# Conditioned hybrid layer: the first norm's row weighing, tile turns and column sums put in another order

## The reference

```
cond = silu(c)                                   # one vector of 1024
mod  = cond @ ada_w + ada_b                      # 6*1024 columns
sh1, sc1, g1, sh2, sc2, g2 = split(mod, 6)
hn   = rmsnorm(x, norm1_g) * (1 + sc1) + sh1     # x is (2048, 1024)
u    = hn @ w_in                                 # gate branch and x branch
x_br = causal_dwconv(x_br, conv_w, conv_b)       # 4 taps along the tokens
r, i = sigmoid(xb @ wa + ba), sigmoid(xb @ wx + bx)   # 8 blocks of 128 channels
h_t  = a_t * h_(t-1) + sqrt(1 - a_t^2) * i * xb  # a = exp(-8 r softplus(-lambda))
```

## Time and profile before

| | us |
|---|---|
| median of 3 runs | 1262.37 |
| the three runs | 1267.21, 1262.37, 1259.74 |
| the profiled execution, its own time | 1262.1 |
| its span in the trace | 1260.4 |

### The profile page before, as it was taken

The page is one execution under the profiler, slowest core; times in us unless marked ns, Lnnn a source line. Parts: engine busy times, 40 slices in busy tenths (PEclk is TensorE's granted clock), DMA queues, the critical chain, the costliest instruction groups (busy, mean ns, idle before and its releaser), DMA issues. The chain is left out here.

```text
span 1260.4 us, 18928 instructions
## 1 busy us (share of the span) xinstructions
PE 1093.1 (87%) x4857; PEld 850.4 (67%) x4858; DVE 768.6 (61%) x1198; ACT 650.0 (52%) x900; POOL 611.9 (49%) x665
## 2 busy tenths in 40 slices
PE   2797999999999997379999992599799999999991
PEld 2686788888888885368888871476466666766660
DVE  3477866667657664536677778356456655656541
ACT  3988766776677666322222212255556655555541
POOL 0061726637447340022567767146555655666553
PEclk9788999999999999689999995699999999999996
DMA  9550334433343312661445627857687887776751
GB/s 362 194 193 29 107 102 135 154 117 121 118 156 118 117 51 83 220 231 69 152 179 189 234 118 267 271 191 252 222 297 245 288 299 245 261 250 231 246 168 51
DMA packets 130871, 231.00 MB, mean 183 GB/s; under 512 B 24104, under 2 KB 91776, under 8 KB 129296
## 3 DMA queue, kind: packets, MB, share of 16 engines
q1 hardware_dynamic: 88976, 118.15, 28.2%
q0 software_dynamic: 23632, 62.49, 13.5%
q10 hardware_dynamic: 18224, 49.90, 11.6%
HBM read 175.87 MB, written 91.31 MB: 212 GB/s over the span
## 5 line engine op out<-in xcount | busy, mean ns | idle before, releaser
L1687 PE MATMUL po<-w_dn,e_ah 128*128 (+1 forms) x312 | 147.1, 616 | 16.9 <-issue 8.9
L1666 PE MATMUL pl<-w_hi,e_xh 128*128 (+1 forms) x312 | 140.9, 452 | 11.8 <-DVE e_xl L1577 6.3
L1210 PE MATMUL po<-wo_hi,b_yh 128*128 128x512 f32 x256 | 105.0, 410 | 28.0 <-DVE wo_lo L1024 28.0
L1668 PE MATMUL pl<-w_hi,e_xl 128*128 (+1 forms) x312 | 124.7, 400 | 0.0
L1667 PE MATMUL pl<-w_lo,e_xh 128*128 (+1 forms) x312 | 124.0, 397 | 0.0
L558 DVE SCALAR_TENSOR_TENSOR XB<-xu,v_cols,XB 128x512 f32<-128x512 f32 x96 | 90.1, 939 | 43.2 <-ACT XB L336 39.5
L1687 PEld LDWEIGHTS po<-w_dn,e_ah 128*128 128x128 f32 x312 | 57.9, 195 | 80.0 <-issue 80.0
L1377 POOL TENSOR_TENSOR e_ob<-e_obs,e_fg 128x1024 f32<-128x1024 f32 x38 | 91.1, 2397 | 32.2 <-ACT e_obs L1495 32.2
L674 PE MATMUL pg<-hT_hi,wg_hi 128*128 128x512 f32 x256 | 103.1, 403 | 0.0
L1211 PE MATMUL po<-wo_lo,b_yh 128*128 128x512 f32 x256 | 101.6, 397 | 0.0
L1212 PE MATMUL po<-wo_hi,b_yl 128*128 128x512 f32 x256 | 101.6, 397 | 0.0
(11 more groups left out here) (287 smaller groups left out, 2637.4 us busy)
## 6 DMA issues: line engine op xcount, KB each, us to landing
e_xg<-hn_slots ACTq DMA_DIRECT2D x40, 512.0 KB, 5.4
e_xa<-x_slots ACTq DMA_DIRECT2D x38, 512.0 KB, 3.8
stg<-in_ada_w_dram POOLq DMA_DIRECT2D x32, 512.0 KB, 4.2
w_raw<-in_moe_w_down_dram SPq DMA_DIRECT2D x16, 1024.0 KB, 7.3
w_raw<-in_moe_w_gate_dram SPq DMA_DIRECT2D x32, 384.0 KB, 4.3
w_raw<-in_moe_w_up_dram SPq DMA_DIRECT2D x32, 384.0 KB, 5.7
n_ada<-in_ada_w_dram ACTq DMA_DIRECT2D x4, 2048.0 KB, 18.4
hn_slots<-in_x_dram SPq DMA_DIRECT2D x16, 512.0 KB, 5.4
```

Of the source, the lines that this page charges most:

```text
L1210: nc.tensor.matmul(po[u][:, hcols], yh[u][:, tok], wo_hi[:, k, hcols], start=(k == 0), stop=False)
L1666: nc.tensor.matmul(gu[:], xh[:, tok], hi, start=(k == 0), stop=False)
L1668: last = nc.tensor.matmul(gu[:], xl[:, tok], hi, start=False, stop=(k == KD - 1))
L1687: last = nc.tensor.matmul(dst, ah[:, k * P:(k + 1) * P], rows, start=(k == 0), stop=(k == KF - 1))
```

## The change

Nothing is computed otherwise; calls change places in four of the engines' lists, and one overlay moves.

- DVE: the eight `weigh` are spread less: 1 to 7 stand among the diagonals 0 to 4 and are all done before diagonal 5; before, 5 to 7 stood among the diagonals 5 to 9. The diagonals 14 and 15 go into the first pass of the channel loop.
- PE: the column sums stand behind turn 4 (before: turn 9). Turns 5 to 7 follow, then the first projection; 8 and 9 behind it, 10 and 11 behind the second, 12 to 15 behind the first gate projection.
- ACT: `squares` and `evacuate` take the places that this asks for; group 0 is finished after `squares(8)` (before: `squares(13)`), the squares 13 to 15 and evacuations 10 to 15 lie in the first pass, groups 2 and 3 both at its end.
- There are four diagonals in a ring instead of two, over `macc` instead of `XBh`. So POOL, whose sums write `macc`, waits for turn 15 before its first one. It did not wait for turns before.

```diff
-        vrow, diag = over("v_rows", [VROWS * KD, P], "mtmp"), over("n_diag", [P, 2, P], "XBh")
+        vrow, diag = over("v_rows", [VROWS * KD, P], "mtmp"), over("n_diag", [P, NDIAG, P], "macc")
...
             def diagonal(it):
...
-                if it >= 2:
-                    dve.wait_ge(turned, it - 1)
+                if it >= NDIAG:
+                    dve.wait_ge(turned, it - NDIAG + 1)
...
@@ ACT @@
+            squares(7)
+            squares(8)
             finish_group(0)
-            for it in range(14, NT):
-                evacuate(it - 4)
+            for it in range(5, 8):
+                evacuate(it)
+            for it in range(9, 12):
                 squares(it)
             finish_group(1)
-            evacuate(12)
-            evacuate(13)
+            act.wait_ge(s_b, 1)
+            nc.scalar.activation(sp_t[:, 3], sp_t[:, 2], ACT.Ln).then_inc(s_a, 1)
...
+            evacuate(8)
+            evacuate(9)
+            squares(12)
...
                     if begins and h == 0:
-                        evacuate(14)
-                        evacuate(15)
+                        squares(13)
+                        evacuate(10)
+                        evacuate(11)
+                        squares(14)
...
-                        finish_group(2)
+                        squares(15)
+                        for it in range(12, NT):
+                            evacuate(it)
...
                     if begins and h == 0:
+                        finish_group(2)
                         finish_group(3)
@@ POOL @@
             load(0, 0)
             load(0, 1)
+            pool.wait_ge(turned, NT)
@@ PE @@
-            for it in range(10):
+            for it in range(5):
                 turn(it)
             pe.wait_ge(acc_step, KD)
...
-            turn(10)
-            turn(11)
+            for it in range(5, 8):
+                turn(it)
...
-                            turn(12 + 2 * n)
-                            turn(13 + 2 * n)
+                            turn(8 + 2 * n)
+                            turn(9 + 2 * n)
...
                         project("g", pg[n], (h * NH + n) * NB).then_inc(g_mm, 1)
+                        if h == 0 and n == 0 and not at_least(j, 1):
+                            for it in range(12, NT):
+                                turn(it)
                         gates(h, n)
```

More of the change, by code:

```diff
@@ L94, in norm_and_lru @@
         macc = sb("macc", [P, NB])
+        XT = ("A", "T", "M", "GE", "TI")
+        XR, NDIAG = len(XT), 4
         acc = over("n_acc", [P, 2 * D], "stg")
-        vrow, diag = over("v_rows", [VROWS * KD, P], "mtmp"), over("n_diag", [P, 2, P], "XBh")
-        XT = ("A", "T", "M", "GE", "TI")
+        vrow, diag = over("v_rows", [VROWS * KD, P], "mtmp"), over("n_diag", [P, NDIAG, P], "macc")
         xt = [over("n_x_" + n, [P, D], n) for n in XT]
@@ L262, in _ @@
                 squares(it)
-            for it in range(4, 14):
-                evacuate(it - 4)
[L265 to L281, removed]
+            evacuate(0)
+            squares(4)
+            evacuate(1)
+            convert("x", 0)
+            evacuate(2)
+            squares(5)
+            evacuate(3)
+            convert("g", 0)
+            act.wait_ge(gw_in, 32)
+            nc.scalar.activation(gwh[:], gw[:], ACT.Copy).then_inc(gw_hi_done, 1)
+            squares(6)
+            act.wait_ge(vec_ready, 1)
+            nc.scalar.activation(sp_t[:, 0], lam, ACT.Abs).then_inc(s_a, 1)
+            act.wait_ge(s_a, 1)
+            nc.scalar.activation(sp_t[:, 1], sp_t[:, 0], ACT.Exp, scale=-1.0).then_inc(s_a, 1)
+            evacuate(4)
+            squares(7)
+            squares(8)
             finish_group(0)
-            for it in range(14, NT):
-                evacuate(it - 4)
+            for it in range(5, 8):
+                evacuate(it)
+            for it in range(9, 12):
                 squares(it)
             finish_group(1)
-            evacuate(12)
-            evacuate(13)
+            act.wait_ge(s_b, 1)
+            nc.scalar.activation(sp_t[:, 3], sp_t[:, 2], ACT.Ln).then_inc(s_a, 1)
+            act.wait_ge(cond_ready, 1)
+            nc.scalar.activation(xu[:, 0, 0:CONV - 1], zero[:], ACT.Copy).then_inc(halo_ready, 1)
+            evacuate(8)
+            evacuate(9)
+            squares(12)
             def gates_out(c, n, j):
@@ L463, in _ @@
             nc.vector.tensor_copy(vec[:].rearrange("p r k -> p (r k)"), pg[0][:, 0:VROWS * KD]).then_inc(vec_ready, 1)
+            weigh(1)
             diagonal(0)
-            weigh(1)
+            weigh(2)
             diagonal(1)
-            weigh(2)
+            weigh(3)
             diagonal(2)
+            weigh(4)
+            weigh(5)
             diagonal(3)
-            weigh(3)
             diagonal(4)
+            weigh(6)
+            weigh(7)
             low_weights("x", 0)
-            weigh(4)
             diagonal(5)
+            low_weights("g", 0)
+            low_gates(0)
             diagonal(6)
+            columns()
+            diagonal(7)
+            finish_group(0)
+            for it in range(8, 12):
+                diagonal(it)
             dve.wait_ge(s_a, 2)
             nc.vector.tensor_scalar(sp_t[:, 2], sp_t[:, 1], 1.0, None, ALU.add).then_inc(s_b, 1)
[L478 to L489, removed]
+            finish_group(1)
             diagonal(12)
             diagonal(13)
-            finish_group(1)
-            diagonal(14)
-            diagonal(15)
             dve.wait_ge(s_b, 1)
@@ L584, in body @@
                     low_xb(c, 0)
+                    if begins and h == 0:
+                        diagonal(14)
                     if before:
@@ L588, in body @@
                     if begins and h == 0:
-                        finish_group(2)
+                        diagonal(15)
                     if h == 1 and not last:
@@ L652, in turn @@
                 for k in range(KD):
-                    last = nc.tensor.matmul(pt[it % 2][:, k * P:(k + 1) * P], xt[it % XR][:, k * P:(k + 1) * P], diag[:, it % 2],
+                    last = nc.tensor.matmul(pt[it % 2][:, k * P:(k + 1) * P], xt[it % XR][:, k * P:(k + 1) * P], diag[:, it % NDIAG],
                                             start=True, stop=True)
```

3 lines of the change are left out of this document (1 added, 2 removed).

## The result

| | before | after |
|---|---|---|
| median of 13 runs each, same chip, us | 1259.74 | 1265.49 |
| lowest to highest | 1252.02 to 1267.21 | 1260.35 to 1272.26 |
| the profiled execution, its own time | 1262.1 | 1272.26 |
| its span | 1260.4 | 1270.5 |

The ratio after to before is 1.0055, 95% interval 1.0031 to 1.0079: the kernel became slower, by 6.9 us (3.9 to 10.0); the two medians lie 5.75 us apart. I had predicted 1261.2 us and no measurable difference. The time of 1265.49 us lies inside the range that I gave (1255.5 to 1268), but the kernel moved where I had said that it would not: the interval excludes 1, and the loss stands at about the 0.5% that I had called too little to measure. The chance that I gave to slower was 0.08.

What follows compares the result with a forecast made beforehand. ACT was taken to bound the head's end: groups 2 and 3 end at 118.0 instead of 119.05, plus 24.6 us gives 142.6 for the second pass; 1262.1 less 1.0 is 1261.1, forecast 1261.2 us, range 1255.5 to 1268.

Steps and rivals of the forecast that it cites:

- What bounds the kernel: PE sets the pace from the second pass on; ACT bounds the head's end, with 24.6 us from 119.05 to 143.6.
- Start of group 0: ACT begins group 0 at 48.2 instead of 66.93, 18.7 us earlier.
- First projection: PE's first projection, behind turn 7 at 3.7 us, starts at 60.1, 13.2 us earlier than 73.30.
- First gates: PE's first gates start at 97.4 as turns 14 and 15 hang on evacuation 12; 1.5 of 13.2 us are left.
- Groups 2 and 3: ACT's groups run from 101.9 to 118.0, with POOL beside DVE, against 119.05 before: 1.0 us earlier.
- the taps at 1.7 times: Bound: DVE slowed beside POOL by the taps' ratio in groups 2 and 3; ACT ends near 124.2, kernel 1267.3 us.
- The tail: From ACT's end of group 3 to the second pass, 24.6 us as before, giving 142.6 instead of 143.6.
- POOL's sums: POOL's first pass ends at 121 to 125, hidden if before 129.1, some 4 us of cover.
- rival 2: POOL is late for `mod_sum`, ending at 136.6; second pass 7.5 us later, kernel 1269.6 us; chance 0.06.
- Rivals 1 and 3: 1: early projection's 13.2 us stay, 1249 us, chance 0.11. 3: sums stay put as condition rows come late, 1266, chance 0.05.
- The rule of the Trainium skill: GpSimd contends with VectorE instructions of two SBUF inputs or two-port mode; taken alone, it gives ACT's end at 119.3.
- The clock: PE's idle gaps before turns 7 and 14 bring the lower clock; full clock there wins 1.8 us each, 1257.5 us.

Runs made afterwards that it cites:

- e2: After, with the four diagonals over `TR` instead of `macc` and POOL's sums begun early, without a wait for turns; ratio to before 1.0012.
- e3: After, with the diagonals over `TR` and POOL's sums waiting for group 1's low parts instead of turn 15; ratio to before 1.0027.
- e4: Before, with one line added: POOL waits for turn 15 before its first sum; ratio to before 0.9979.
- e7: After, with evacuations 5, 12, 13, squares 15 and diagonals 14, 15 moved earlier, diagonals over `TR`, POOL's sums early without the wait; ratio to before 0.9961.
- e8: The closed-up order of turns with diagonals over `TR`, but POOL's sums wait for turn 15 as in after; ratio to before 1.0004.
- e10: The closed-up order of turns with diagonals over `TR`, POOL's sums waiting for group 0's low parts; ratio to before 0.9975.
- e5: After, with the diagonals over `TR` instead of `macc` but POOL still waiting for turn 15; ratio to before 1.0065.
- e1: After, with POOL's first pass cut to 8 of 512 columns behind its first step; only the head is read, ratio to before 1.0091.
- e6: After, with the additions of POOL's first pass cut to 8 columns, scalings at full width; only the head is read, not timed.
- e9: After, with POOL's first-pass scalings behind the first cut to 8 columns, additions at full width; only the head is read, not timed.

## Why the prediction was wrong, step by step

- *What bounds the kernel*: right. PE is busy for all of 150 to 200 us in after too, so what the head loses is kept. The head's 4.8 us (at the second pass's first gates) stand beside 6.9 (3.9 to 10.0) in the ratio. For e2 it is 0.3 beside 1.5, for e3 1.9 beside 3.4, for e4 0.3 beside -2.6, for e7 -6.75 beside -4.9, for e8 0.5 beside 0.5, for e10 -4.4 beside -3.1, each within the ratio's interval. e5's 3.6 beside 8.2 (5.2 to 11.2) is outside, which stays open. The two profiled executions differ by 10.1 us; the 5.3 beyond the head come after 165 us. From the second pass's first gates to the end before needs 1100.4 us and after 1105.7, but e5, which is as slow as after, 1096.0, and e4, in before's order, 1106.3: that looks like scatter from one execution to the next.
- *Start of group 0*: predicted 48.2, measured 48.23.
- *First projection*: predicted 60.1, measured 59.77, with turn 7 at 3.75 us (taken: 3.7).
- *First gates*: predicted 97.4, measured 95.97. Most of the 1.4 us comes from the twelve small decay operations, priced at 3.45 us by a row of before with POOL at work beside them; in after, with POOL idle, they take 1.71 (82.14 to 83.85). That turn 14 hangs on evacuation 12 fits the trace: its row names DVE's reciprocal, but that is tile 15's, diagonal 14 had been done since 87.96, and ACT's evacuations 12 and 13 ran from 89.62. In e7, with evacuation 12 further ahead, turn 14 follows turn 13 without idle and the first gates are at 91.15.
- *Groups 2 and 3*: this is the step that failed, in one term. Their place was right (predicted 101.9 for the start, measured 100.65), the gap before the second gates went as said. But the price of POOL beside DVE was taken as a factor 1.19, less half for slack, which put 1.5 us on the 116.5 worked out for ACT alone. The factor is 1.88 for the subtractions and 1.97 for the scalings; the slack that DVE has without the sums, 1.4 us in e1, is used up (no gap from 101.63 to 115.3). The sums cost 6.5 us, from 116.06 in e1 to 122.57, where 118.0 had been predicted. e1's 116.06 beside the 116.5 says that the rest of the working was sound.
- *Why I took 1.19*: the 821 ns are the mean of a window that has one whole addition of POOL in it (82.45). DVE's timeline of before over that window had the price, had I looked at single rows: beside the addition two subtractions take 2.38 us, in front of it two take 1.33.

```profile
80.55 1.33 DVE L451 TENSOR_TENSOR hT_lo<-n_zT,hT_hi 128x512 fp32r<-128x512 f32 x2 [1.73 <-ACT hT_hi L257]
...
82.57 2.38 DVE L451 TENSOR_TENSOR hT_lo<-n_zT,hT_hi 128x512 fp32r<-128x512 f32 x2
```

The row nearer in kind was in my bounds: the taps at 1.7 times, which gave 124.2 and 1267.3. The window of those taps in before has POOL busy for 3.56 of 3.90 us:

```profile
93.20:97.10 3.90, 3.90 (x18) 3.19 (x17) 3.83 (x4) 0.55 (x1) 3.56 (x4) 1.00 0.40 134
```

Three operations beside a POOL in full work are closer to the new stage than eight subtractions beside a POOL that waits for a DMA. I took the value near the milder row because it was the same line of the code, where it should have been the one with the same neighbour.
- *The tail*: a second, smaller term that was off. I kept 24.6 us from the tanh to the end of the fourth gates, that is 23.1 to their start. Measured 24.4, 1.3 us more. All kernels in the new order have 24.2 to 24.5 there, wherever their first sums lie (e1: 24.26), and the two in the old order, before and e4, 23.1 and 23.0. POOL's second pass also begins sooner behind the tanh, 4.1 us in after (126.71) and 8.8 in before (127.87), and DVE's taps and scan are longer beside it; that this is the cause no run shows. With the 4.6 us at the tanh it makes the 5.9 by which the second pass missed its predicted start (142.6, measured 148.5). DVE's timeline of after, then of before:

```profile
131.00 3.83 DVE L564 SCALAR_TENSOR_TENSOR XB<-xu,v_cols,XB 128x512 f32<-128x512 f32 x3 [2.54 <-ACT XB L341]
...
136.91 3.38 DVE L553 TENSOR_TENSOR_SCAN M<-A,T 128x1024 f32<-128x1024 f32 x1
```

```profile
127.50 2.96 DVE L558 SCALAR_TENSOR_TENSOR XB<-xu,v_cols,XB 128x512 f32<-128x512 f32 x3 [2.59 <-ACT XB L336]
...
133.22 2.28 DVE L547 TENSOR_TENSOR_SCAN M<-A,T 128x1024 f32<-128x1024 f32 x1
```

- *POOL's sums and rival 2*: POOL began at 96.43 and its last addition ended at 117.4, before `mod_sum` at 125.51, which kept within the cover that ended at 129.1. I looked at POOL only as someone who might be late. It cost time by being there.
- *Rivals 1 and 3*: the early projection did not carry through (13.5 us at the first projection are 2.9 at the first gates), and the change does what it says.
- *The rule of the Trainium skill*, GPSIMD Engine Reference, section Key points, that GpSimd contends with VectorE's instructions of two SBUF inputs or a two-port mode: this case's runs agree with it for the subtractions, which have two SBUF inputs, and far more strongly than the pair of means that I had set beside it: 688 ns became 1292, and e1 took it back to 690. The scalings, with one, went from 542 to 1070; in which mode they ran no run shows. The page gives no size.
- *The clock*: turns 7 and 14 ran at the lower level in after, as the bound took it, but the idle time in front does not settle it. e6 has the same order up to there and 2.48 us idle, and its turn 14 ran at the full clock (PE's timeline of e6); in e5 it was 2.65 us idle and 2.02 us. Both reach the first gates 1.1 to 1.6 us before after does.

```profile
90.78 2.02 PE L664 MATMUL n_pt<-n_diag,n_x_TI 128*128 128x128 f32 x16 [2.48 <-DVE n_rstd L432]
```

## What to carry to other kernels

When a change moves one engine's work under another's, price the pairing by a row in which that neighbour is fully at work, and count its operations in the window before using a mean. Ask of an engine that comes under a stage not only whether it is late but what it does to the others there. Where such work has slack, give it a place beside a stage that waits for something else: against a head without them (e1), the sums cost 6.7 us beside the two groups that load DVE most (after), and 2.1 us where they start early (e2). How much a place costs depends on the order around it: in the old order, where DVE had more pauses there, moving the sums under the same two groups cost 0.3 us (e4).

## What the runs showed of the hardware that I had not expected

- Eight of DVE's subtractions (128x512, f32) beside POOL's alternating scalings and additions took 1292 ns on average, 1.88 times the 688 of a stretch without POOL. DVE's busy time for the same 25 operations of groups 2 and 3 was 14.67 us with POOL's work cut to slivers (e1), 16.25 beside five scalings (e6), 19.87 beside six additions (e9), and 22.67 beside six of each (after).
- POOL loses less. Its scalings have a mean of 865 ns beside the groups in after, against 0.69 us at 96.43 where DVE was idle, and its additions 1438 against 1.29 (98.07): by these figures 1.8 us in that stretch, an estimate.
- PE's idle time alone did not say which clock followed. 2.82 us idle stands before fourth gates at the full clock in after (146.99) and at the lower level in e8 (139.85) and e9 (143.54), and turn 14 took 3.53 us behind 2.49 idle in after and 2.02 behind 2.48 in e6.
